# Projecting dilated-attention values with tokens on the partitions in a float32r decoder trunk

## What is computed

```
hn  = rmsnorm(h, norm_mix[0])
qkv = (hn @ w_qkv).reshape(B, T, 3 groups, 3 (q,k,v), 16 heads, 64)
for each group g: o_g, l_g = dilated_group_attention(q_g, k_g, v_g, window_g, dilation_g)
o   = sum_g softmax_g(l_g) * o_g
h   = h + o @ w_o
```

## Time and profile before

| | |
|---|---|
| median of 3 runs | 1652.12 us |
| the profiled execution, its own time | 1652.47 us |
| its span on the core | 1650.7 us |
| granted TensorE clock, mean | 0.997 of full speed |
| TensorE matmuls (PE) busy | 98% |
| TensorE weight loads (PEld) busy | 81% |
| VectorE (DVE) busy | 56% |
| ScalarE (ACT) busy | 37% |
| DMA, mean rate | 97 GB/s |

### The profile page before, as it was taken

One profiled execution on the slowest core, in us unless ns is written; L12 is line 12 of the kernel. 1 busy time (PEld: TensorE's weight loads), 2 busy tenths in 40 slices (PEclk: granted clock), 3 DMA queues, 4 the chain that ended last, 5 costly groups with the idle time before them and its releaser, 6 DMA issues.

```text
span 1650.7 us, 22246 instructions
## 1 busy us (share of the span) xinstructions
PE 1622.1 (98%) x8323; PEld 1332.5 (81%) x8323; DVE 921.8 (56%) x1632; ACT 608.0 (37%) x1058; POOL 59.6 (4%) x58
## 2 busy tenths in 40 slices
PE   7999999999999899999999999999999999999998
PEld 5888888888888688888888878888868888888887
DVE  5454554554555763545455676777776354545555
ACT  5234234234233432222223444665553122222344
POOL 0000000000000200000001110000020000000111
PEclk9999999999999999999999999999999999999999
DMA  5543443443332233333333332323223333333332
GB/s 142 145 121 90 109 121 88 109 120 83 97 85 69 83 96 102 89 102 93 99 98 92 105 113 77 90 63 98 58 74 102 101 91 102 89 102 89 102 102 78
DMA packets 308312, 159.66 MB, mean 97 GB/s; under 512 B 31156, under 2 KB 303085, under 8 KB 308254
## 3 DMA queue, kind: packets, MB, share of 16 engines
q1 hardware_dynamic: 308092, 158.85, 34.0%
q10 hardware_dynamic: 162, 0.03, 0.0%
HBM read 156.64 MB, written 10.60 MB: 101 GB/s over the span
## 4 chain that ended last, share of the span: by engine, by line
PE 94%; DVE 3%; ACT 1%; POOL 1%; DMA 1%; issue 0%; SPq 0%; POOLq 0%; ACTq 0%
PE unit_out L1455 28%; PE unit_out L1457 27%; PE unit_out L1456 27%; PE turned L1531 2%; PE attn L1589 2%; PE attn L1816 1%; PE logits L1455 1%; PE misc L1531 1%; PE logits L1531 1%; POOL sumsq L740 1%; PE logits L1457 1%; PE logits L1456 1%; DMA w_raw<-in_a_w_qkv_dram 1%; PE logits L1571 1%; DVE act_lo L1050 1%; DVE heads L1242 0%
## 5 line engine op out<-in xcount | busy, mean ns | idle before, releaser
L1455 PE MATMUL unit_out<-act_hi,w_hi 128*128 128x512 f32 (+1 forms) x2032 | 805.6, 396 | 11.7 <-DVE act_lo L1050 8.9
L1457 PE MATMUL unit_out<-act_hi,w_lo 128*128 128x512 f32 (+1 forms) x2032 | 790.9, 389 | 0.0
L1456 PE MATMUL unit_out<-act_lo,w_hi 128*128 128x512 f32 (+1 forms) x2032 | 790.3, 389 | 0.0
L1455 PEld LDWEIGHTS unit_out<-act_hi,w_hi 128*128 128x128 f32 x2032 | 382.4, 188 | 100.8 <-DVE act_lo L1050 9.9
L1457 PEld LDWEIGHTS unit_out<-act_hi,w_lo 128*128 128x128 f32 x2032 | 381.7, 188 | 79.8
L1456 PEld LDWEIGHTS unit_out<-act_lo,w_hi 128*128 128x128 f32 x2032 | 382.2, 188 | 77.4 <-issue 2.4
L755 ACT ACTIVATE w_hi<-w_raw 128x1024 fp32r<-128x1024 f32 (+3 forms) x259 | 274.0, 1058 | 440.5 <-PE unit_out L1457 362.9
L1035 DVE TENSOR_TENSOR w_lo<-w_raw,w_hi 128x1024 fp32r<-128x1024 f32 (+3 forms) x259 | 324.0, 1251 | 104.9 <-ACT w_hi L755 104.9
L896 ACT ACTIVATE act_hi<-hidden 128x512 fp32r<-128x512 f32 x64 | 40.5, 633 | 243.4 <-DVE hidden L1261 243.4
L740 POOL TENSOR_TENSOR sumsq<-sumsq,square 128x512 f32<-128x512 f32 x41 | 57.5, 1403 | 1576.0 <-ACT square L776 1574.3
L1258 DVE TENSOR_TENSOR scaled<-unit_out,rstd 128x512 f32<-128x512 f32 x64 | 44.1, 690 | 67.7 <-PE unit_out L1457 67.7
(11 more groups left out here) (231 smaller groups left out, 1152.6 us busy)
## 6 DMA issues: line engine op xcount, KB each, us to landing
w_raw<-in_w_ff_dram SPq DMA_DIRECT2D x128, 512.0 KB, 4.0
w_raw<-in_a_w_qkv_dram SPq DMA_DIRECT2D x72, 512.0 KB, 3.8
w_raw<-in_b_w_qkv_dram SPq DMA_DIRECT2D x24, 512.0 KB, 5.1
w_raw<-in_w_ple_gate_dram SPq DMA_DIRECT2D x16, 512.0 KB, 4.1
bias_tiles_b<-bias_vectors SPq DMA_DIRECT2D x16, 256.0 KB, 4.3
bias<-bias_tiles_b SPq DMA_DIRECT2D x8, 512.0 KB, 3.8
w_raw<-in_a_w_o_dram SPq DMA_DIRECT2D x8, 448.0 KB, 3.7
w_raw<-in_b_w_o_dram SPq DMA_DIRECT2D x8, 384.0 KB, 3.4
```

The source lines that it names most:

```text
L1455: te.matmul(bank, w_k[0], hi, start=start, stop=False)
L1456: te.matmul(bank, w_k[0], lo, start=False, stop=False)
L1457: return te.matmul(bank, w_k[1], hi, start=False, stop=stop)
```

## The change

The values of groups 1 and 2 are projected the other way round: the activations of 128 tokens are stationary, and the weights of two pairs, 256 columns, move. The result has the tokens on the partitions, so it is not turned and not copied by ScalarE. Group 0 keeps its unit, its turn and its copy. Since two pairs are made at once, the values of a group take two units in a row in every odd step (half 0 for the first 4 chunks of input features, half 1 for the last 4), which fill both banks of `unit_out`, and none in an even step. In their place an even step projects group 0's and group 1's query of the next pair (the third number in `A_ORDER`). The number of units stays 72.

```diff
-A_ORDER = [(0, V), (1, V), (2, V), (0, Q), (0, K), (1, Q), (1, K), (2, Q), (2, K)]
-A_UNITS = len(A_ORDER)
+A_ORDER = ([(0, V, 0), (0, Q, 0), (0, K, 0), (1, Q, 0), (1, K, 0), (2, Q, 0), (2, K, 0), (0, Q, 1), (1, Q, 1)],
+           [(1, V, 0), (1, V, 1), (2, V, 0), (2, V, 1), (0, V, 0), (0, K, 0), (1, K, 0), (2, Q, 0), (2, K, 0)])
+A_TURN_V = [order.index((0, V, 0)) + 1 for order in A_ORDER]
...
+                if kind == V and g:
+                    first = (g * 3 + kind) * D + (pair.const - 1) * P
+                    load(u, wa[:, n * KV:(n + 1) * KV, first:first + 2 * P], wide_weights(w_raw[u.const % 2]))
...
+                if has_proj and A_ORDER[par][i][1] == V and A_ORDER[par][i][0]:
+                    g, _, half = A_ORDER[par][i]
+                    if half:
+                        for n in range(2):
+                            if n == 0:
+                                wait(ve, values_half, (s - 1).half().times(GROUPS - 1) + g)
+                            else:
+                                wait(ve, units_done, u + 1)
+                            bank = unit_out[(u.const - 1 + n) % 2]
+                            ve.tensor_tensor(
+                                a_values(g, n),
+                                bank[:, :].rearrange("p (a h c) -> p a h c", a=2, h=2),
+                                start_scale[:, 2 * n:2 * n + 2].unsqueeze(2).unsqueeze(3).to_broadcast([P, 2, 2, P]),
+                                ALU.mult).then_inc(evac_done, 1)
...
+            def values_unit(u, g, kind, half):
+                w = u.const % 2
+                wait(te, lo_done, u + 1)
+                for a in range(NT):
+                    bank = unit_out[(u.const - half + a // 2) % 2][:, a % 2 * BLK:(a % 2 + 1) * BLK]
+                    if half == 0 and a % 2 == 0:
+                        wait(te, evac_done, u - 1 + a // 2)
+                    for k in range(KV):
+                        hi, lo = (x[:, half * KV + k, a * P:(a + 1) * P] for x in IN[0])
+                        w_k = [wide_weights(x[w])[:, k, :] for x in (w_hi, w_lo)]
+                        te.matmul(bank, hi, w_k[0], start=half == 0 and a % 2 == 0 and k == 0, stop=False)
+                        te.matmul(bank, hi, w_k[1], start=False, stop=False)
+                        last = te.matmul(bank, lo, w_k[0], start=False,
+                                         stop=half == 1 and a % 2 == 1 and k == KV - 1)
+                    if half == 1 and a == 1:
+                        last.then_inc(values_half, 1)
+                last.then_inc(units_done, 1)
...
-                if has_proj and 1 <= i <= GROUPS:
+                if has_proj and i == A_TURN_V[par]:
                     wait(te, evac_done, u)
-                    wait(te, v_ready, s.times(GROUPS) + (i - 1))
+                    wait(te, v_ready, s)
                     turn(misc, [(a * P, a_v_t(i - 1)[:, a * P:(a + 1) * P])
                                 for a in range(NT)]).then_inc(vt_ps, 1)
```

More of the change, by code:

```diff
@@ L58 @@
 V, Q, K = 2, 0, 1
-A_ORDER = [(0, V), (1, V), (2, V), (0, Q), (0, K), (1, Q), (1, K), (2, Q), (2, K)]
-A_UNITS = len(A_ORDER)
+A_ORDER = ([(0, V, 0), (0, Q, 0), (0, K, 0), (1, Q, 0), (1, K, 0), (2, Q, 0), (2, K, 0), (0, Q, 1), (1, Q, 1)],
+           [(1, V, 0), (1, V, 1), (2, V, 0), (2, V, 1), (0, V, 0), (0, K, 0), (1, K, 0), (2, Q, 0), (2, K, 0)])
+A_TURN_V = [order.index((0, V, 0)) + 1 for order in A_ORDER]
+A_UNITS = len(A_ORDER[0])
+KV = KC // 2
 A_PAIRS = HEADS // 2
@@ L366, in a_v_t, with a_made, a_splits, a_values @@
             return (scaled, hidden)[i % 2][:, :]
+        def a_made(par, i):
+            g, kind, ahead = A_ORDER[par][i]
+            return (par + ahead) % 2, g, kind
+        def a_splits(par, i):
+            return i > 0 and A_ORDER[par][i - 1][0] == 0 and A_ORDER[par][i - 1][1] != V
+        def a_values(g, half):
+            pairs = heads[:, :].rearrange("p (par x t) -> p par x t", par=2, t=T)
+            return pairs[:, :, g * 3 + V, half * BLK:(half + 1) * BLK].rearrange("p h (a c) -> p a h c", c=P)
+        def wide_weights(w):
+            return w[:, 0:KC, :].rearrange("p (k n) c -> p k (n c)", n=2)
         def b_v_t(par):
@@ L470, in build @@
         v_ready = sem("v_ready")
+        values_half = sem("values_half")
         scores_ready = sem("scores_ready")
@@ L583, in _, with load @@
                 load_x(c)
-            def load(u, src):
+            def load(u, src, dst=None):
                 par = u.const % 2
                 wait_apart(sp, lo_done, u - 1, (s_sel, 16))
-                sp.dma_start(w_raw[par][:, 0:min(KC, width_of(u)), :], src
+                sp.dma_start(w_raw[par][:, 0:min(KC, width_of(u)), :] if dst is None else dst, src
                              ).then_inc(raw_ready[par], 16)
@@ L594, in load_a @@
             def load_a(pair, u, i):
-                g, kind = A_ORDER[i]
-                load(u, wa[:, :, bass.ds((pair.times(P) + (g * 3 + kind) * D).v, P)])
+                g, kind, n = A_ORDER[pair.const % 2][i]
+                if kind == V and g:
+                    first = (g * 3 + kind) * D + (pair.const - 1) * P
+                    load(u, wa[:, n * KV:(n + 1) * KV, first:first + 2 * P], wide_weights(w_raw[u.const % 2]))
+                else:
+                    first = (g * 3 + kind) * D + (pair.const + n) * P
+                    load(u, wa[:, :, first:first + P])
             load_a(At(0), At(0), 0)
@@ L840, in sub_a @@
                     e.then_inc(exp_done, 1)
-                if has_proj and i in (4, 5):
-                    split_qk_hi(a_parts(par, A_ORDER[i - 1][1]), a_product(i - 1), u)
-                if has_proj and 1 <= i <= GROUPS:
-                    wait(sc, vt_ps, s.times(GROUPS) + i)
-                    sc.activation(a_buf(par, i - 1, V), misc[:, :], ACT.Copy).then_inc(v_ready, 1)
+                if has_proj and a_splits(par, i):
+                    to, _, kind = a_made(par, i - 1)
+                    split_qk_hi(a_parts(to, kind), a_product(i - 1), u)
+                if has_proj and i == A_TURN_V[par]:
+                    wait(sc, vt_ps, s + 1)
+                    sc.activation(a_buf(par, 0, V), misc[:, :], ACT.Copy).then_inc(v_ready, 1)
                 if has_attn and i == A_UNITS - 1:
@@ L965, in sub_b @@
                 if has_scores and i == 0:
-                    wait(sc, vt_ps, s + GROUPS * A_PAIRS)
+                    wait(sc, vt_ps, s + A_PAIRS)
                     sc.activation(b_buf(1 - par, V), misc[:, :], ACT.Copy).then_inc(v_ready, 1)
@@ L1183, in sub_a @@
                     scale_a(s, i)
-                if has_proj and i in (4, 5):
-                    split_qk_lo(a_parts(par, A_ORDER[i - 1][1]), a_product(i - 1), s.times(2) + (i - 3))
-                if has_proj:
+                if has_proj and a_splits(par, i):
+                    to, _, kind = a_made(par, i - 1)
+                    split_qk_lo(a_parts(to, kind), a_product(i - 1), s.times(2) + (2 * (to - par) + kind + 1))
+                if has_proj and A_ORDER[par][i][1] == V and A_ORDER[par][i][0]:
[4 more added lines that the diff above has]
+                                wait(ve, values_half, (s - 1).half().times(GROUPS - 1) + g)
+                            else:
+                                wait(ve, units_done, u + 1)
[5 more added lines that the diff above has]
+                                ALU.mult).then_inc(evac_done, 1)
+                elif has_proj:
                     if start:
                         start_statistics()
[L1189 to L1192, removed]
+                    to, g, kind = a_made(par, i)
+                    dst = a_v_t(i) if kind == V else a_product(i) if g == 0 else a_buf(to, g, kind)
                     src, by = unit_out[u.const % 2][:, :], (rstd_q if kind == Q else rstd)[:, :]
@@ L1629, in sub_a @@
                     start = s.reg is None and s.const == 0 and i < 2
-                    if not start:
+                    if A_ORDER[par][i][1] == V and A_ORDER[par][i][0]:
+                        values_unit(u, *A_ORDER[par][i])
+                    elif not start:
                         whole(u, IN[0])
@@ L1745, in head_squares @@
                 if has_scores:
-                    wait(te, v_ready, s + GROUPS * A_PAIRS)
+                    wait(te, v_ready, s + A_PAIRS)
                 wait(te, osq_ready, s - 1)
```

## The result

The changed kernel took 1659.24 us as the median of 6 runs (1658.48 to 1660.05), the kernel before 1652.08 (1651.77 to 1654.23, 6 runs). The ratio is 1.0042, with a 95% interval of 1.0031 to 1.0053: slower by 0.42%, where 0.14% less was forecast and the range ended at 1654.5. The profiled execution took 1658.48 us with a span of 1656.7, 6.0 us more than the span before.

A forecast was written before the change was run, and what follows sets the result against it. TensorE's instruction stream alone was taken to bound the mixer. Fewer turns, -7.1 us, plus halved matmuls, +4.8, gave -2.3; from the profiled 1652.47, less 0.35 for the median, the forecast was 1649.8 us, range 1646.5 to 1654.5.

The forecast's parts named there:

- What bounds the kernel now: Mixer steps, 61.95 us each: only TensorE's instruction stream sets the time, so each microsecond added or removed shows in full.
- Changed: sixteen units: Odd steps' new value units: 48 matmuls of 256 columns replace 24 of 512, 0.1198 us apart, +4.8 us in all.
- Rival 3: New units: stationary load, 0.19 us, no longer hidden in the 0.12 us slot; +73 us, 1723 us; chance 0.01.
- Turns: Transposes of values in mixer steps: 16 fewer at 0.44 us each, -7.1 us.
- rival 1: Wide units dearer than the last unit's rows: at 0.126 us a matmul 1654.6 us; chance of over +0.2% 0.10.
- rival 4: New units: fixed part of a matmul mostly hidden; at zero the sum is -7.1, 1645.0 us; chance 0.07.
- rival 5: Mixer steps: a turn is worth near 0.52 us, sum -3.5, 1648.6 us; chance 0.08.
- gap rule: Matmul streams: warm distance N/2.4 plus about 2.5 ns; would make the halved matmuls cost 1.0 us, result 6.1 us faster.
- overlap rule: New units: a stationary load runs beside matmuls in flight only when its row group differs; speaks against the change.
- Evacuations: VectorE, odd steps: two behind every half 1, 1.8 us of slack; added waits and the broadcast scale priced at nothing.
- rival 2: TensorE waits for the evacuation behind half 1, slots 2 and 4 of odd steps; 1 us each gives 1657.8; chance 0.05.
- The queues: SyncE's weight loads keep size and place, in pieces twice as long; bias loads and tile expansions keep theirs.

The follow-up runs named there:

- experiments on the head's place: Loop's first instruction moved within its 256-instruction code block: changed kernel to number 0, 1650.84 us, to number 64, 1662.0 us; kernel before to number 200, 1662.71 us.
- the halves with the hint: Kernel before, units of slots 0 to 3 of odd steps in two 256-column halves, plus an instruction announcing TensorE's jump back: 1657.48 us, ratio 1.0025.
- three ways: Changed kernel with TensorE's loop written out, 1650.99 us; with an instruction announcing the jump back, 1650.74; with the loop starting a code block, 1650.84.
- the hint ahead of the jump: Changed kernel, loop kept, with an instruction at its top that announces the jump back: 1650.74 us, ratio 0.9989.
- writing the loop out: TensorE's hardware loop over steps 1 to 6 unrolled: changed kernel 1650.99 us, ratio 0.9989; kernel before, as control, 1652.28 us, ratio 0.9998.
- the head at number 0: Changed kernel with the first instruction of TensorE's loop moved to the start of a 16 KB code block: 1650.84 us in one run.
- all five kernels that stalled: Changed kernel 1659.24 us, its loop start at 64 1662.0; kernel before with odd-step units halved in slots 0-3 1664.27, slots 0-1 1662.45, loop start at 200 1662.71.
- the head-at-200 kernel: Kernel before, same instructions in the loop, with TensorE's loop beginning at number 200 of a 256-instruction code block: 1662.71 us, ratio 1.0061.
- four slots in halves: Kernel before with units of slots 0 to 3 of the odd steps issued in two halves of 256 columns: 1664.27 us, ratio 1.0067.

## Why the prediction was wrong

**Where it failed.** The step is in "What bounds the kernel now": "within the mixer nothing but TensorE's own stream of instructions sets the time". The windows showed only that this held for a loop of 784 matmuls. The term "Changed: sixteen units" then priced 384 added matmuls by what the array does with them, 13 ns each, and not by what their instructions do to the loop that holds them. With 80 more matmuls (96 in four units, less 16 transposes of four turns) and as many loads in its body, TensorE's loop touches 8 blocks of code in the place of 7. At each of its two jumps back TensorE stands still for 2.4 to 2.5 us while a block of code is loaded, and behind one of them the lower clock costs 2.88 us more. That is 7.8 of the 8.3 us between the forecast's -2.3 and the 6.0 measured. The experiments on the head's place show it from both sides, with the body's instructions unchanged: 8.4 us less on the changed kernel in one run (9.2 where each is held against the kernel before on its own chip), and 11.0 more on the kernel before.

No rival had it, and so the range was too short. Rival 3 came near in words, with a load that is no longer hidden, but it meant the stationary load, and that stayed hidden: 0.12 us spacings while a weight load of the same shape takes 0.19.

**Turns.** Right. Even steps fell by 61.95 - 61.05 = 0.90 where 0.89 was forecast. They lose two turns and add no matmul, so this is the price of a turn by itself, 0.45.

**The wide units.** Right, 0.1199 for 0.1198. The odd steps have 62.24 to 62.25 for 62.27, and the halves with the hint gave 4.6 us for the 4.8. Rivals 1, 4 and 5 fell with these numbers. The gap rule (which its section gives for a single matmul and not for a stream) and the overlap rule of the Trainium skill ("TensorE: Matmul & The Clock Gate", sections "Back-to-back issue gap" and "What overlaps and what doesn't") are not borne out here: 119.9 ns against the first's 109.2, and the hidden loads of 128 rows against the second.

**The seams.** From the last unit matmul at 84.91 to the scores at 85.12 are 0.21 us for the 0.3 forecast.

**Evacuations.** Right: TensorE waits for none of them (rival 2), and the broadcast scale costs nothing. VectorE's two evacuations of slots 0 and 1 in step 1 (start, us, idle before), to be held against the earlier trace rows:

```profile
82.35 0.69 DVE L1224 TENSOR_TENSOR heads<-unit_out,start_scale 128x512 f32<-128x512 f32 x1 [0.56 <-PE unit_out L1649]
85.23 0.69 DVE L1224 TENSOR_TENSOR heads<-unit_out,start_scale 128x512 f32<-128x512 f32 x1 [2.18 <-PE unit_out L1649]
```

**The queues.** The loads of weights were priced at nothing. The changed kernel's profile has 0.83 us of late ones in steps 0 and 1. Other kernels with the same loads show none in their one profile, so it is no sure cost of the change.

With the loop out of the way the sum holds: 1650.99, 1650.74 and 1650.84 us (this in one run) in three ways, 1.6 to 2.1 us under the kernel before of the same chip, for the 2.3 forecast. That is within 0.2% of no change, as forecast: the turns give 7.1 and the halved matmuls take 4.8 back. The price of the loop is what the forecast lacked. Not tried was moving 512 columns (four pairs) at a time, which would avoid the 4.8 but wants four banks.

## What to carry to other kernels

Before you add instructions to a hardware loop, count its body on the busiest engine in blocks of code, with the place of its head, and look at the "instruction" packets of a window inside the loop, from its second round on: none means that it stays loaded, nine from one jump back to the next went here with a wait at every jump. Where it doesn't fit, the hint ahead of the jump, a head at a block's start, or writing the loop out gave 8 to 9 us here. An idle time put down to "issue" at the head of a loop is the sign, and a change of a few instructions to a loop near its limit should carry such a case in its range.

## What the runs showed of the hardware that I had not expected

- On TensorE a loop that touches 7 blocks of 16 KB ran round after round with no load of code (none in two rounds, in the kernel before and with the head at number 0), and all five kernels that stalled loaded 9 from jump to jump; their loops touch 8, by the count of instructions and the place of the head where it was set. The Trainium skill has it otherwise: "Advanced Engine Details and Errata", section "ISA Cache", says there are only two lines of 16 KB, and "Runtime: NRT & Kernel Launch", section "Instruction fetch mechanics", that a taken branch to a target outside the two-page window waits for a load. By that the kernel before would stall as well; it doesn't. That a jump to code that isn't there waits, the runs bear out: 2.4 to 3.1 us.
- With the hint even 8 blocks stay loaded. The reading that fits the packets: without it TensorE loads one block past the loop's end ahead of the jump (at 191.62 us in the changed kernel), a ninth, and that pushes out the block of the loop's head. With the hint this packet is absent and nothing is loaded again. That the ninth takes the place of the head is inferred from the order of the packets; the trace doesn't say which block a packet holds.
- Loading code in sequence costs TensorE nothing: 14 blocks in 250 us, and no idle time.
- An idle time of 2.4 to 3.1 us was sometimes followed by a stretch at the 1.2 GHz level and sometimes not. In the changed kernel the clock fell behind 2.36 us (for 6.6 us, 2.88 lost) but not behind 2.52; in the head-at-200 kernel behind both; with four slots in halves behind 2.83 (about 1.5 lost) but not behind 2.58. What tells these apart stays open. Where it happens, it can double the price of a stall.
